# A two-layer decoder step: last expert rounds combined in PSUM, second-layer rounds in another order, and filled edges

## What is computed

```
x = LN(alpha * x + mixer(x))          layer 0: pooling + retention; layer 1: forgetting attention
x = LN(alpha * x + memattn(x, mem))
x = LN(alpha * x + hier_moe(x))
hier_moe: p_grp, grp = top_k(softmax(x @ w_gc + b_gc), 1)
          top_val, top_idx = top_k(fine logits of that group, 2)
          h = silu(x @ w_gate[e]) * (x @ w_up[e])
          y = sum over the two experts e of gate[e] * h @ w_down[e]
```

## Time and profile before

| | |
|---|---|
| median of three runs | 1575.76 us (1575.52 to 1583.64) |
| the profiled execution | 1572.08 us |
| its span | 1570.3 us |
| PE busy | 1444.2 us (92%) |
| DVE, ACT, POOL busy | 564.4 (36%), 323.2 (21%), 218.3 us (14%) |
| moved by DMA | 357.68 MB, mean 228 GB/s |

### The profile page before, as it was taken

The page is one execution under the profiler, slowest core; times in us unless marked ns, Lnnn a source line. Parts: engine busy times, 40 slices in busy tenths (PEclk is TensorE's granted clock), DMA queues, the critical chain, the costliest instruction groups (busy, mean ns, idle before and its releaser), DMA issues.

```text
span 1570.3 us, 21504 instructions
## 1 busy us (share of the span) xinstructions
PE 1444.2 (92%) x8419; PEld 961.4 (61%) x8419; DVE 564.4 (36%) x1203; ACT 323.2 (21%) x755; POOL 218.3 (14%) x249
## 2 busy tenths in 40 slices
PE   8999999999988999989999989989999984989990
PEld 7888888875764333357888864448875762323330
DVE  1631334423373111124534336753515175111115
ACT  0111211222041111114100035530223032111112
POOL 0000000000003332232410000000000002343354
PEclk9999999999999999999999989999999996989995
DMA  8211422454476999875368697942435255989863
GB/s 310 79 54 58 147 95 98 170 215 164 185 289 240 368 390 397 326 308 212 141 229 335 238 341 286 391 179 79 184 108 215 107 209 206 371 337 395 345 191 120
DMA packets 86286, 357.68 MB, mean 228 GB/s; under 512 B 23081, under 2 KB 26697, under 8 KB 59681
## 3 DMA queue, kind: packets, MB, share of 16 engines
q1 hardware_dynamic: 51376, 274.34, 45.9%
q0 software_dynamic: 24512, 46.99, 8.8%
q10 hardware_dynamic: 10297, 34.97, 5.6%
HBM read 408.16 MB, written 33.11 MB: 281 GB/s over the span
## 4 chain that ended last, share of the span: by engine, by line
PE 83%; DVE 7%; DMA 3%; ACT 3%; issue 3%; SPq 1%; POOL 0%; ACTq 0%; POOLq 0%; DVEq 0%
PE PS L639 78%; PE PS L1198 2%; DMA MKV<-in_moe_w_gu,OVR 1%; DVE EX L1279 1%; PE PS L726 1%; DMA W<-in_mem_kt 1%; PE PS L975 1%; PE PS L1220 1%; ACT X L1961 1%; DMA W<-in_fox_v 1%; DVE TOK L1883 0%; DVE TOK L1884 0%; SPq L510 0%; DMA W<-in_ab_w_in 0%; ACT X L1948 0%
## 5 line engine op out<-in xcount | busy, mean ns | idle before, releaser
L639 PE MATMUL PS<-X,W 128*128 128x260 f32 x1264 | 289.5, 386 | 11.0 <-DMA W<-in_ab_w_in 6.8
L639 PEld LDWEIGHTS PS<-X,W 128*128 128x128 f32 x1264 | 239.5, 191 | 51.7 <-issue 10.7
L639 PE MATMUL PS<-O,W 128*128 128x260 f32 x1024 | 228.4, 383 | 2.4 <-DVE O L1669 1.6
L639 PEld LDWEIGHTS PS<-O,W 128*128 128x128 f32 x1024 | 193.7, 190 | 36.9 <-issue 3.4
L1899 ACT ACTIVATE BIG<-PS 128x512 f32<-128x512 f32 (+2 forms) x161 | 75.0, 467 | 301.9 <-PE PS L639 183.7
L639 PE MATMUL PS<-W,BIG 128*64 128x512 f32 x512 | 116.5, 609 | 2.0 <-DVE BIG L1802 2.0
L2381 POOL TENSOR_TENSOR SM<-SM,O 128x5 f32<-128x5 f32 x2 | 0.4, 194 | 788.6 <-DVE SM L1747 788.6
L1807 DVE SCALAR_TENSOR_TENSOR BIG<-BIG,SM,PS 128x256 f32<-128x256 f32 x32 | 15.4, 481 | 246.9 <-ACT BIG L2244 239.8
L639 PE MATMUL PS<-MKV,BIG 128*64 128x512 f32 (+1 forms) x384 | 91.4, 525 | 1.4 <-ACT BIG L1899 1.0
L1272 DVE SCALAR_TENSOR_TENSOR X<-X,PS 128x260 f32<-128x260 f32 x64 | 27.1, 423 | 148.9 <-PE PS L639 148.9
L639 PEld LDWEIGHTS PS<-W,BIG 128*64 128x64 f32 x512 | 36.5, 140 | 71.0 <-issue 71.0
(11 more groups left out here) (331 smaller groups left out, 1743.3 us busy)
## 6 DMA issues: line engine op xcount, KB each, us to landing
W<-in_moe_w_gu SPq DMA_DIRECT2D x64, 1024.0 KB
TMP<-in_moe_w_down SPq DMA_DIRECT2D x32, 1024.0 KB
W<-in_fox_kt SPq DMA_DIRECT2D x64, 512.0 KB, 5.7
W<-in_fox_v SPq DMA_DIRECT2D x64, 512.0 KB, 6.6
W<-in_mem_kt SPq DMA_DIRECT2D x16, 1024.0 KB, 9.2
W<-in_cache_mem_v SPq DMA_DIRECT2D x16, 1024.0 KB, 8.5
y_rows<-BIG ACTq DMA_DIRECT2D x32, 512.0 KB
W<-in_mem_wkv SPq DMA_DIRECT2D x13, 1024.0 KB, 4.8
```

Of the source, the lines that this page charges most:

```text
L639: return nc.tensor.matmul(out, lhsT, rhs, start=start, stop=stop, **kw)
```

## The change

1. Start: X and weight block 0 arrive in four parts of two k-steps; PE runs two output tiles of the first half side by side over the parts (`first_groups`); the order of the first four groups is tile 0, tile 1, then both again for the second half. The clearing of PSUM is in two pieces.
2. Value rows: four of the ten transposed groups stay before the attention loop, on banks 0 to 3. The others go into its steps 1, 6, 7 and 8 (`ROW_STEPS`). `fox_v_sample` is stored in step 1, `fox_v` after step 8, and POOL's load of the new value rows waits for both.
3. Edges: `fox_o` runs 7 of 8 k-steps of its first three groups, and `mo0`/`mo1` 6 of 8 of their first two, before the last tiles of `O` are there. Banks are rotated to allow it.
4. Round order in layer 1: 0, 1, 8, 2, 9, 3, 10, ... 7, 14, 15. `y_rows` is indexed by round, so that the slot needs no renumbering and three linked steps of DVE in the router go.
5. Tail: the last two rounds (14 and 15) are not stored; PE adds their rows to the tokens with one-hot matrices (`last_hot`, `last_rows`) in PSUM, and DVE adds PSUM. POOL adds all other rows by DMA after its last round, first slots, then second slots; the late fetches go.

```diff
-ROUNDS = (0, 8, 1, 9, 2, 10, 3, 11, 4, 12, 5, 13, 6, 14, 7, 15)
+ROUNDS = ((0, 8, 1, 9, 2, 10, 3, 11, 4, 12, 5, 13, 6, 14, 7, 15), (0, 1, 8, 2, 9, 3, 10, 4, 11, 5, 12, 6, 13, 7, 14, 15))
...
+ROW_BANK = (0, 1, 2, 3, 0, 1, 1, 0, 1, 0)
+ROW_STEPS = {1: (4, 5), 6: (6,), 7: (7,), 8: (8, 9)}
...
-        SOON = (NR - 4) * P
+        SOON = (NR - 2) * P
...
+            def first_groups():
+                for i in range(FIRST_PARTS):
...
+                    for pos in range(2):
+                        group("ab_in", pos, X, part=range(2 * i, 2 * i + 2))
...
+                        for q in ROW_STEPS.get(v, ()):
+                            value_rows(q)
                         if v in hooks:
                             hooks[v]()
+                        if v == 31:
+                            pe.wait_ge(S("fa_out"), 7)
+                            group("fox_o", 0, O, part=range(KT - 1))
+                        if v == 32:
+                            pe.wait_ge(S("sa_out"), 4)
+                            group("fox_o", 1, O, part=range(KT - 1))
+                    group("fox_o", 2, O, part=range(KT - 1))
...
+                    if u == 18:
+                        pe.wait_ge(S("ma_out"), 8 * l + 6)
+                        pe.wait_ge(S("s_weights"), 5 * l + 2)
+                        group(f"mo{l}", 0, O, part=range(KT - 2))
+                pe.wait_ge(S("s_turned"), 5 * l + 1)
+                group(f"mo{l}", 1, O, part=range(KT - 2))
...
+                def last_rows(t, q):
+
+                    if q == 0 and t == 4:
+                        pe.wait_ge(S("last_hot"), 2 * NT)
+                    if q == 0 and t == 3:
+                        pe.wait_ge(S("z_mv"), NT + 1)
+                    if t == 4:
+                        pe.wait_ge(S("y_A"), 2 * NR - 1 + q)
+                        pe.wait_ge(S("y_V"), 2 * NR - 1 + q)
+                    w = P if t < NCH else NS
+                    for n in range(2):
+                        last = mm(bank(TAIL_BANK[t] + n)[0:w, :], LAST_HOT[:, q, t * P:t * P + w], YB[:, q, n * 512:(n + 1) * 512], q == 0, q == 1)
+                    if q == 1:
+                        last.then_inc(S("dn_acc"), 1)
...
                     if i:
+                        if l == 1 and i == NR:
+                            last_rows(4, 0)
                         down(i - 1)
                     if i < NR:
                         hidden(i)
+                if l == 1:
+                    last_rows(4, 1)
+                    for t in range(NCH):
+                        for q in range(2):
+                            last_rows(t, q)
...
-            V.memset(bank(0, 8), 0.0).then_inc(S("ps_zero"), 1)
+            V.memset(bank(0, 2), 0.0).then_inc(S("ps_zero"), 1)
+            V.memset(bank(2, 6), 0.0).then_inc(S("ps_zero"), 1)
...
-                link(V.tensor_scalar(A12, R12, FIXED - 0.5, -float(P * (NR - 1)), ALU.is_gt, ALU.mult))
-                link(V.scalar_tensor_tensor(SL, R12, float(P), SL, ALU.mult, ALU.add))
-                link(V.tensor_tensor(SL, SL, A12, ALU.add))
...
-                link(V.tensor_scalar(A12, SL, float(SOON), 65536.0, ALU.is_lt, ALU.mult))
+                if l == 1:
+                    V.tensor_scalar(LAST_TOK, EB2[:, NR - 2:NR], -1.0, None, ALU.add)
...
-                    dve.wait_ge(S(f"yg{t}"), 96)
+                    dve.wait_ge(S(f"yg{t}"), 64)
+                    dve.wait_ge(S("dn_acc"), 4 * NR + n + 1)
                     z = XT[0:w, t, :]
-                    link(V.scalar_tensor_tensor(z, fetched(l, t, 1), 1.0, z, ALU.mult, ALU.add, accum_out=row(n, 0)))
+                    link(V.scalar_tensor_tensor(z, bank(TAIL_BANK[t], 2)[0:w, :], 1.0, z, ALU.mult, ALU.add, accum_out=row(n, 0)))
...
-                    act.dma_start(y_rows[l][i * P:(i + 1) * P, :], YB[:, q, :]).then_inc(S(f"st_y{q}"), 16)
+                    if l == 0 or i < NR - 2:
+                        r = ROUNDS[l][i]
+                        act.dma_start(y_rows[l][r * P:(r + 1) * P, :], YB[:, q, :]).then_inc(S(f"st_y{q}"), 16)
...
-                    add = l == 1 and c == 0
+                    add = l == 1
...
-                    if l == 1 and i == NR - 2:
-                        pool.wait_ge(S("x_scaled"), NT)
-                        for q in range(2):
-                            pool.wait_ge(S(f"st_y{q}"), 16 * (NR // 2 + 6))
-                        for t in ORDER:
-                            fetch(t, 0, SLOT, SOON)
...
+                else:
+                    pool.wait_ge(S("pool_step"), pool_steps[0])
+                    for q in range(2):
+                        pool.wait_ge(S(f"st_y{q}"), 16 * (NR // 2 + 7))
+                    for c in range(2):
+                        for t in ORDER:
+                            if c == 1:
+                                pool.wait_ge(S(f"yg{t}"), 48)
+                            fetch(t, c, SLOT, SOON)
```

More of the change, by code:

```diff
@@ L85, in __init__ @@
             b = pos % 2 if beside_retention(name, pos) else pos % 4
+            if name == "fox_o":
+                b = (0, 2, 3, 1)[pos % 4]
+            if name in ("mo0", "mo1"):
+                b = (2, 3, 0, 1)[pos % 4]
             if name == "fox_in" and pos >= 4:
@@ L639, in mm, with group @@
                 return nc.tensor.matmul(out, lhsT, rhs, start=start, stop=stop, **kw)
-            def group(name, pos, src, n=HALF):
+            def group(name, pos, src, n=HALF, part=range(KT)):
                 g, m, h = PROJ.groups(name)[pos]
[L643 to L648, removed]
+                if part[0] == 0:
+                    if g >= 2:
+                        pe.wait_ge(*arrived(PROJ.block0[name] + m // 2))
+                    if PROJ.prev[g] is not None:
+                        wait_evac(pe, PROJ.count[PROJ.prev[g]])
                 w = Wl[PROJ.slot[PROJ.block0[name] + m // 2]]
                 b = bank(PROJ.bank[g])
[L651 to L654, removed]
+                for k in part:
                     if name in ("kv0", "kv1") and m >= 8:
@@ L945, in _, with value_rows @@
                         seven(b, hooks)
-                    wait_out(pe, "fox_in")
+                    def value_rows(q):
+                        g, t = divmod(q, 6)
+                        if q == 0:
+                            wait_out(pe, "fox_in")
+                        if q == 7:
+                            pe.wait_ge(S("fa_out"), 1)
+                        before = [p for p in range(q) if ROW_BANK[p] == ROW_BANK[q]]
+                        if before:
+                            pe.wait_ge(S("fv_out"), before[-1] + 1)
+                        for f in range(4):
+                            src = TMP[:, 4 * (t - NCH) + f, SEQ:T] if t >= NCH else TMP[:, 4 * g + f, t * P:(t + 1) * P]
+                            n = src.shape[1]
+                            last = nc.tensor.transpose(bank(ROW_BANK[q])[0:n, f * P:(f + 1) * P], src, ident)
+                        last.then_inc(S("fv_t"), 1)
+                    for q in range(NCH):
+                        value_rows(q)
                     pe.wait_ge(S("new_out"), 1)
[L948 to L951, removed]
                     pe.wait_ge(S("qk_out"), 4)
@@ L2137, in _ @@
                                     5: lambda: (put_flipped(2), put_flipped(3))}
+                    for q in range(NCH):
+                        put_rows(q)
                     for v in range(33):
@@ L2436, in _ @@
                         gather(i + 3)
[L2437 to L2443 removed]
+                    v = ROUNDS[l][i - 1] - FIXED if i else -1
                     if 0 <= v < FIXED - 1:
```

138 lines of the change are left out of this document (83 added, 55 removed).

## The result

| | before | changed |
|---|---|---|
| device time, median of 20 runs each, us | 1577.15 (1568.62 to 1583.64) | 1583.41 (1577.13 to 1593.88) |
| changed over before, 95% interval | | 1.0048 [1.0034, 1.0063] |
| profiled execution, us | 1572.08 | 1585.16 |
| its span, us | 1570.3 | 1583.5 |

The change costs 7.6 us by the ratio and 13.1 us between the two profiled executions; I had summed +1.1. The time lies in the range, and the ratio just under the 0.5% bound, but that is no credit to the sum, which is 6.5 us short, and the parts are further off than the total.

A forecast was written before the change was run, and what follows sets the result against it. TensorE (PE) was taken to bound the kernel outside the last 37 us, with DMA equally in layer 1's attention. Terms summed to +1.1 us: 1573.2 profiled, 1577 us against the runs' median; 8-in-10 range 1563 to 1587.

The forecast's parts named there:

- Start: Kernel start: first wait covers a quarter of the data, a later short wait goes; -1.9 us, ends 0 and -3.
- Value rows: Layer 1 attention: scores start sooner, but store and fetch run into the page stream; +2.5 us, ends -1.8 and +6.5.
- Router: Router before the first gather: one DVE step less on the path, once a layer; -0.4 us, ends 0 and -1.6.
- Filled edges: Output projections: early k-steps fill PE's waits; -3.6 us in fox_o, -2.0 in mo0 and mo1 together.
- Round order: Layer 1's rounds: overflow loads late, waits of 1.4 us (round 9) and 7.0 (round 10); +2.5 us, ends -9.7 and +8.
- Rival A: Layer 1's rounds: loads of rounds 9 and 10 get an even DMA share, arrive in time; 1565 us, chance 0.22.
- Two overflow rounds last: Before round 15: its empty loads come late, 1.8 us wait before gate and up; 2.4 before down, off the path.
- rival C: New short waits lower the clock, 3.1 us for each of three on the path; 1586 us, chance 0.14.
- Tail: After the last rounds: adding fetches put DVE's first big add at 1551.9 against 1548.21; +4.0 us, ends -9 and +8.

The follow-up runs named there:

- values_only: The kernel before with only the fox value rows written as in the change; ratio to before 1.0043 [1.0022, 1.0064].
- moe_only: The kernel before, keeping its start, edges and value rows, with the change's rounds, row storage and tail; ratio to before 1.0072 [1.0047, 1.0098].
- start_edges: The kernel before with the start in four parts and the filled edges, without the value rows; ratio to before 0.9946 [0.9920, 0.9972].
- order_first: The change with before's alternation of layer 1's rounds up to round 13, rounds 14 and 15 still last; ratio to before 0.9999 [0.9983, 1.0016].
- ln_early: The change with LN's two loads issued some 50 us earlier, behind the last fixed down load; ratio to before 1.0019 [0.9988, 1.0051].
- combo: The change with before's alternation up to round 13, LN's loads early and three adding fetches ahead of overflow_dn(7); ratio to before 0.9942 [0.9912, 0.9973].

## Why the prediction was right or wrong, point by point

**Start.** Right: first product at 4.77 us, 2.0 sooner, and 2.5 at the next cut (in the other traces with this start 0.9 to 2.2).

**Value rows.** The mechanism was right (store and fetch run into the pages, PE follows the DMA), with waits of 2.1 and 3.9 us as foretold. The term was +2.5; the traces show +2.3 to +4.4 and the runs 6.8 with 3.5 as the lower end. What the sum lacked is the low clock behind a wait for pages: 1.7 us more for sixteen records, here (976.43, above) and in values_only.

**Router.** -0.2 in layer 1 does not show: from the 100 records to the first gate and up it takes 69.07 us in moe_only, which has the shorter router, and 69.09 in before.

**Filled edges.** fox_o was undersized (3.6, measured 5.5). The waits that I had counted made the clock fall as well, and without them it stays up. The same stretch of before and of start_edges (columns as above):

```profile
1040.00:1054.00 14.00, 8.83 (x48) 4.55 (x49) 6.09 (x17) 5.28 (x14) 0.00 (x0) 0.88 0.04 5
```

```profile
1030.00:1044.00 14.00, 12.47 (x83) 8.50 (x80) 9.58 (x29) 6.42 (x21) 0.00 (x0) 1.00 0.01 2
```

```profile
1047.07 2.37 PE L649 MATMUL PS<-W,TOK 128*64 128x512 f32 x16
```

The third row is start_edges' last value product: 2.37 us, where before takes 3.96 for the same sixteen records behind its waits. That is 1.6 of the missing 1.9. I had written that after the wait of 2.10 us the next products ran as usual; these rows contradict that. mo0 and mo1 were oversized: -2.0, measured +0.5 and -0.7. I had taken mo0 "as the same" as mo1 without looking at who is late next there; in_cache_mem_v was.

**Round order.** The step failed at the size of each wait: 1.4 us for round 9 and 7.0 for round 10 in the forecast, 5.5 to 6.8 for round 9 and mostly none for round 10 measured. I had 0.136 MB/us for POOL's queue from the earlier trace rows, and from 2 us after the first issue. Queues of the change from 1362 to 1378, and two stretches of it, 1366:1370 and 1374:1378:

```profile
q1 hardware_dynamic: 571, 4.15, 61.8%
q0 software_dynamic: 569, 1.98, 30.5%
q10 hardware_dynamic: 158, 0.58, 8.9%
...
q1 hardware_dynamic: 154, 1.13, 67.1%
q0 software_dynamic: 156, 0.08, 6.9%
...
q1 hardware_dynamic: 192, 1.44, 85.5%
q0 software_dynamic: 188, 0.16, 12.1%
```

The rate is 0.124 MB/us, 9% less, and makes 1.5 us of a load of 15.4. The start is the larger part: issued at 1356.67, the load moved nothing before 1360 and 0.21 MB in 1360:1362, about 2 us later than I had it (1361.5, less the 2.7 by which these rounds start sooner). From about 1361 to its landing at 1379.64 it took 18.6 us. The two stretches show where much of that went. A round's four overflow loads are of 1.05 MB each, but only 2.1 MB move: the second and the fourth are empty. In between, 1362:1366 and 1370:1374, the queue moved 0.82 and 0.91 MB; in these two it had as many packets as SP's queue and hardly a byte. So the empty half of a load takes its turns too, some 4 us each time beside a full queue, and PE waits for the last of them. That is read from the bytes and the order of issue; no run leaves these loads out. The sum (8.4 us of waits, one fall of the clock) came out near the usual trace: C is 191.0 to 191.2 there, +2.8 with round 15's wait, against +4.3. The 197.4 of the change's own trace was the less common case. Rival A is out: the even share did not appear, 61.8% and 30.5% in the rows above. It took from queues served in turn, a packet from each (the Trainium skill, DMA: Bandwidth & Descriptors, Queues, rings and completion order), that the bytes would be even. By the profile's packets the trace agrees with the turns (571 and 569); the packets differ in size.

**Two overflow rounds last.** 1.8 us forecast before round 15, 3.0 measured, with the load landing 3.27 us after its issue where I had 2.0, and 1.6 us of low clock behind it that I had left to rival C. So C was right for this wait of 3.0 us, though not for order_first's of 1.2.

**Tail.** The largest miss: +2.2 from the last gate and up (the +4.0 less the 1.8 above), measured +6.7. The first fetch came as worked out, 3.4 us after the down product that releases it (3.5 forecast). Failed: the 19.0 us from there to the first big add, which were 22.25. ln_early puts 2.8 of these on LN's loads, which I had priced at 2.6 and counted; what I had not counted is the start of the queue. POOL's queue in ln_early, 1534:1536 and 1536:1538:

```profile
q0 software_dynamic: 45, 0.18, 81.8%
...
q0 software_dynamic: 111, 0.40, 104.3%
```

It moves 0.20 MB/us only from 1536 on, 5.6 us after the first fetch's issue (1530.41), where I had 3.0: 2.6 of the missing 3. From 1532 to 1540 it moved 1.02 MB, 0.58 less than at its full rate. The other 1.7 us are the low clock in the last gate and up: 12.24 us for 48 records against 10.51. The rest of the tail is within 0.5 us.

**The total.** +1.1 forecast, +7.6 measured. The front was right as a sum (-5.0 forecast without the router, -5.8 measured) by errors that cancel, which is luck; the experts were not: +6.1 forecast with the router, +11.3 measured. Rival C had the size (1586) and part of the mechanism.

## What to carry to other kernels

When a step is moved in a program that one engine issues, write down what that engine waits for ahead of it: the tail lost more by the wait that the adding fetches inherited than by the bytes they move, and taking out six loads that copy nothing gave 12 us. A load that copies nothing is not free in the middle either: count its turns in a full queue, and who waits for it. Before an idle edge is filled, look at which transfer the next product needs; where the transfer is late next, as in mo0, the edge gives nothing. And before one profile is set against another, cut both at the same products: a stretch that the edit doesn't touch tells how much of the difference is the run's.

## What the runs showed of the hardware that I had not expected

The 728 records of stretch A are the same in all fourteen traces, PE is busy throughout, and they took between 134.69 and 141.35 us: 134.7 in five kernels, 136.4 in three, up to 141.4 in four, with either front. The mean granted clock from 110 to 250 us goes with it, 1.00 in the first trace below (values_only) and 0.95 in the second (moe_only):

```profile
110.00:250.00 140.00, 139.32 (x754) 119.79 (x752) 41.78 (x67) 19.86 (x51) 0.00 (x0) 1.00 0.24 84
```

```profile
110.00:250.00 140.00, 139.32 (x723) 119.28 (x723) 38.21 (x64) 19.85 (x51) 0.00 (x0) 0.95 0.24 84
```

In moe_only it is 0.50 for whole windows with PE busy all the time:

```profile
152.00:156.00 4.00, 4.00 (x25) 3.31 (x22) 2.02 (x6) 0.00 (x0) 0.00 (x0) 0.50 0.00 0
```

So the clock also falls to its lower level (1.2 instead of 2.4 GHz) where TensorE was busy throughout, and that alone moves this kernel by 6.7 us, nearly the 7.9 of the bound for "no change". The Trainium skill (TensorE: Matmul & The Clock Gate, What's actually happening) ties the level to how busy the array has been; these rows show the same busy time at either clock, and the reason stays open.

An indirect load whose indices all lie outside still takes a place: 1.3 us of POOL for each and 2.1 to 3.3 us to land when POOL's queue is otherwise empty, 6.6 behind five adding fetches, and 16.3 beside SP's full queue (the last of round 13's in combo, issued at 1452.99, which PE waited for until 1469.34).
